# Who splits the weight tiles of a two-layer encoder: tiles moved between VectorE, GpSimd and ScalarE

## The chip, the cores and the metric

The kernel runs on one core of a Trainium2 chip. The metric is the device time in microseconds; the median of three runs of the kernel before is 1931.53 us (1929.2, 1931.96 and 1931.53).

## The reference

Two layers over 256 tokens of 1024 channels, all in float32:

```
hn = rmsnorm(x, norm1_g);  q, k, v, hy_in, gates = split(hn @ w_in)
a_out = neighbourhood_attention(rmsnorm(q), rmsnorm(k), v, rpb)      # 8 heads of 64
b_out = hyena_mixer(short_conv(hy_in), filters)                      # long convolution by FFT
x = x + (g0 * (a_out @ w_up_na) + g1 * (b_out @ w_up_hy)) @ w_out    # g0, g1: sigmoid gates
h = rmsnorm(x, norm2_g);  q = h @ peer_wq                            # scores against 2 x 128 subkeys a head
x = x + sum over the 16 chosen experts of each head of weight * gelu(h . u_tab[e]) * v_tab[e]
```

The kernel does not gather experts: it computes `h . u` for all 16384 rows of the first table, weights them by a dense matrix of routing weights, and multiplies by all of the second table.

## The kernel before, in words

**Tiles.** All weights of a layer come as one stream of 328 tiles of 128 x 1024 float32 (512 KB), numbered from 0: 0 to 7 for q and k, 8 to 11 for v, 12 to 23 for the Hyena input, 24 to 39 for the gates (`T_GATE`), 40 to 47 for the two up projections (`T_UP`), 48 to 55 for the output projection (`T_OUT`), 56 to 71 for the expert queries (`T_WQ`), 72 to 199 for the first expert table (`T_U`), and 200 to 327 for the second (`T_VT`). Everything before tile 72 is called the trunk here, 72 to 199 the first-table stage, 200 to 327 the second-table stage.

**Ring.** A tile lives in one of four slots (`RING`): `ring` (float32, where the DMA lands), `w_hi` and `w_lo` (fp16). TensorE multiplies in fp16: each product is w_hi x a_hi + w_hi x a_lo + w_lo x a_hi, three matmuls, so 24 matmuls of 256 columns for a normal tile and 12 of 512 columns for a tile of the second table.

**How a tile is split.** ScalarE makes `w_hi` = fp16(4096 x ring) (`high_part`, L504). The low half is 4096 x ring - w_hi, and there are two ways to it. For tiles 0, 1 and 204 to 327, VectorE does it in one instruction (`low_part`, L897). For tiles 2 to 203, ScalarE scales the ring slot in place (`scale_tile`, L510), and GpSimd then subtracts (`scaled_low`, L462). `POOL_TILES` = 204 is where the one way ends and the other begins.

**What orders the work.** Each engine has one list of instructions, written out by hand, which it does in order and in which it waits on semaphores. A slot goes round in a loop: the DMA of tile t + 4 is issued on SyncE when `w_lo` of tile t is made (`refill`); ScalarE makes `w_hi` of tile t + 4 when it has landed and TensorE is done with tile t (`high_wait`), and in the trunk it does this "behind" whatever it does for the results of tile t (`split_behind`); TensorE starts tile t + 4 when its low half is there (`parts_ready`). One counter, `lo_ready`, counts the low halves of all engines, so that tile order is kept across engines: GpSimd's first tile of a layer waits for VectorE's two, and VectorE's tile 204 waits for GpSimd's 203.

**Around the change in the trunk.** The sum of squares of x goes VectorE, TensorE (`mean_square`), ScalarE (the root, L544), VectorE (`inverse_rms`, L923 and on), and then in four steps between VectorE (`make_h` L958, `h_low` L966) and ScalarE (`norm_high`, L613); TensorE waits for the last of them before the v tiles (L1699). In the gate tiles VectorE does the short convolution (`conv`, L1146 to L1150, three instructions for each of twelve blocks), the scores (L1156, L1159) and the softmax's division (L1167), each waited for by TensorE's transposes (L1786).

**Around the change between the tables.** In the last tiles of the first table ScalarE evaluates gelu (`late_gelu`, L822), splits the next tile, and makes the first four expert columns' high halves (`expert_high`, L813). VectorE multiplies gelu by the routing weight (`store_late`, L1480). GpSimd, after its last weight tile, makes the columns' low halves (`expert_low`, L476). TensorE's first second-table product (L1992) needs the first column's low half and tile 200's low half; its second half needs the stores up to the third last.

## Time and profile before

| | value |
|---|---|
| runs, median | 1931.53 us |
| profiled execution, its own time | 1929.89 us |
| its span, first to last instruction | 1927.8 us |
| PE (TensorE matmul) busy | 1873.0 us, 97% |
| ACT (ScalarE) busy | 1355.3 us, 70% |
| DVE (VectorE) busy | 1218.7 us, 63% |
| POOL (GpSimd) busy | 1035.3 us, 54% |
| mean granted TensorE clock | 0.993 |

The profile names engines PE, PEld (weight loads), DVE, ACT, POOL and SP, and L12 is line 12 of the kernel. Layer 0 runs from 0 to about 961 us, layer 1 from there to the end, with nearly the same pattern.

### The profile page before, as it was taken

How to read it: one execution, taken by the hardware profiler on the slowest of the kernel's cores; microseconds unless marked ns; L12 is line 12 of the kernel's file. 1: busy time of each engine (PE TensorE's matmuls, PEld its weight loads, DVE VectorE, ACT ScalarE, POOL GpSimd, SP SyncE). 2: the span in 40 equal slices, each digit the busy share in tenths (PEclk: the TensorE clock that was granted, in tenths of full speed). 3: DMA queues.
4: the chain of work that ended last, by engine and by line, in shares of the span. 5: the costliest groups of instructions: out<-in, count | busy, mean ns of one | idle time of the engine just before them, and what ended most of it. 6: DMA issues, size and time to landing. Idle time of an engine off the chain costs nothing.

```text
span 1927.8 us, 42946 instructions
## 1 busy us (share of the span) xinstructions
PE 1873.0 (97%) x14238; PEld 1353.3 (70%) x14238; DVE 1218.7 (63%) x2530; ACT 1355.3 (70%) x1929; POOL 1035.3 (54%) x664
## 2 busy tenths in 40 slices
PE   7989999999999999999989899999999989999999
PEld 5777898899998344444457778988999974444444
DVE  5897569777775344444458974796777744444444
ACT  8787988887777455555588879888877765555554
POOL 4655868876667322222256558687776672222221
PEclk8999999999999999999999999999999999999999
DMA  8544656655555566666565446556555555656654
GB/s 265 164 143 142 214 168 201 202 188 173 174 174 167 173 205 203 200 206 200 192 213 167 143 135 227 173 197 201 192 171 167 173 175 175 206 201 202 206 198 140
DMA packets 100324, 357.38 MB, mean 185 GB/s; under 512 B 11744, under 2 KB 13730, under 8 KB 99492
## 3 DMA queue, kind: packets, MB, share of 16 engines
q1 hardware_dynamic: 99828, 354.36, 55.9%
q10 hardware_dynamic: 432, 2.18, 0.3%
q8 instruction: 39, 0.64, 0.1%
q14 instruction: 25, 0.20, 0.0%
HBM read 355.45 MB, written 1.05 MB: 185 GB/s over the span
## 4 chain that ended last, share of the span: by engine, by line
PE 87%; DVE 6%; ACT 5%; issue 2%; DMA 0%; SPq 0%; POOL 0%; DVEq 0%; ACTq 0%; POOLq 0%
PE bank L1992 35%; PE bank L1536 14%; PE bank L1538 14%; PE bank L1540 14%; PE bank L1931 3%; ACT w_hi L504 2%; ACT ring L510 2%; PE bank L1860 1%; DVE arena L1150 1%; DVE arena L1167 1%; PE bank L1911 1%; PE bank L1865 1%; DVE arena L1146 1%; DVE arena L1148 1%; PE bank L1699 0%
## 5 line engine op out<-in xcount | busy, mean ns | idle before, releaser
L462 POOL TENSOR_TENSOR w_lo<-ring,w_hi 128x1024 f16<-128x1024 f32 x404 | 863.9, 2140 | 396.5 <-ACT ring L510 395.9
L504 ACT ACTIVATE w_hi<-ring 128x1024 f16<-128x1024 f32 x654 | 685.0, 1047 | 38.2 <-PE bank L1540 25.2
L1536 PE MATMUL bank<-act_parts,w_hi 128*128 128x256 f16 x2560 | 698.0, 273 | 0.5 <-DVE act_parts L1268 0.5
L1540 PE MATMUL bank<-act_parts,w_lo 128*128 128x256 f16 x2560 | 697.8, 273 | 0.0
L1538 PE MATMUL bank<-act_parts,w_hi 128*128 128x256 f16 x2560 | 697.7, 273 | 0.0
L897 DVE SCALAR_TENSOR_TENSOR w_lo<-ring,w_hi 128x1024 f16<-128x1024 f32 x250 | 306.3, 1225 | 351.7 <-ACT w_hi L504 351.7
L476 POOL TENSOR_TENSOR e_lo<-arena,e_hi 128x256 f16<-128x256 f16 x256 | 171.2, 670 | 480.9 <-ACT e_hi L813 480.9
L510 ACT ACTIVATE ring<-ring 128x1024 f32<-128x1024 f32 x404 | 424.2, 1050 | 0.0
L1992 PE MATMUL bank<-w_hi,e_hi 128*128 128x512 f16 x1024 | 390.3, 381 | 11.3 <-issue 11.3
L1992 PE MATMUL bank<-w_lo,e_hi 128*128 128x512 f16 x1024 | 390.2, 381 | 0.0
L1992 PE MATMUL bank<-w_hi,e_lo 128*128 128x512 f16 x1024 | 389.9, 381 | 0.0
L813 ACT ACTIVATE e_hi<-arena 128x256 f16 (+1 forms) x256 | 105.9, 416 | 318.8 <-PE bank L1992 318.8
L1536 PEld LDWEIGHTS bank<-act_parts,w_hi 128*128 128x128 f16 x2560 | 250.4, 98 | 37.9 <-issue 6.4
L1540 PEld LDWEIGHTS bank<-act_parts,w_lo 128*128 128x128 f16 x2560 | 250.4, 98 | 28.9
L1538 PEld LDWEIGHTS bank<-act_parts,w_hi 128*128 128x128 f16 x2560 | 250.5, 98 | 28.4
L1992 PEld LDWEIGHTS bank<-w_hi,e_hi 128*128 128x128 f16 x1024 | 100.6, 98 | 133.5 <-issue 14.3
L1992 PEld LDWEIGHTS bank<-w_hi,e_lo 128*128 128x128 f16 x1024 | 100.7, 98 | 122.2 <-issue 2.5
L1992 PEld LDWEIGHTS bank<-w_lo,e_hi 128*128 128x128 f16 x1024 | 100.6, 98 | 121.5 <-issue 1.9
L1472 DVE SCALAR_TENSOR_TENSOR arena<-arena,bank 128x512 f32 (+1 forms) x128 | 79.4, 683 | 72.8 <-PE bank L1931 72.8
L822 ACT ACTIVATE bank<-bank 128x256 f32<-128x256 f32 x136 | 50.0, 368 | 104.0 <-PE bank L1540 98.1
L1536 PE MATMUL bank<-raw_hi,w_hi 128*128 128x256 f16 x352 | 97.4, 277 | 3.0 <-POOL w_lo L462 3.0
L1540 PE MATMUL bank<-raw_hi,w_lo 128*128 128x256 f16 x352 | 97.4, 277 | 0.0
(258 smaller groups left out, 1862.1 us busy)
## 6 DMA issues: line engine op xcount, KB each, us to landing
ring<-stream SPq DMA_DIRECT2D x654, 512.0 KB, 3.3
arena<-rpb_in SPq DMA_DIRECT2D x8, 512.0 KB, 6.2
arena<-subkeys ACTq DMA_DIRECT2D x2, 1024.0 KB, 5.6
ring<-stream SPq DMA_DIRECT2D x4, 256.0 KB, 4.8
xT<-x_in SPq DMA_DIRECT2D x4, 256.0 KB, 5.2
arena<-w_in SPq DMA_DIRECT2D x2, 512.0 KB
arena<-decay_in SPq DMA_DIRECT2D x2, 512.0 KB
arena<-dft_in SPq DMA_DIRECT2D x2, 512.0 KB, 4.3
```

The costliest lines, as they stand in the source:

```text
L462: pool.tensor_tensor(w_lo[:, slot, :], ring[:, slot, :], w_hi[:, slot, :], ALU.subtract).then_inc(lo_ready.sem, 1)
L476: pool.tensor_tensor(e_lo[:, n % RING, :], experts[:, bass.ds(i * RING + n, 1), :].rearrange("p a t -> p (a t)"), e_hi[:, n % RING, :], AL ...
L504: nc.scalar.activation(w_hi[:, slot, :], ring[:, slot, :], ACT.Copy, scale=TABLE_SCALE).then_inc(hi_ready.sem, 1)
L510: nc.scalar.activation(ring[:, slot, :], ring[:, slot, :], ACT.Copy, scale=TABLE_SCALE).then_inc(ring_scaled.sem, 1)
L813: nc.scalar.activation(e_hi[:, n % RING, :], experts[:, bass.ds(i * RING + n, 1), :].rearrange("p a t -> p (a t)"), ACT.Copy).then_inc(e_h ...
L897: V.scalar_tensor_tensor(w_lo[:, slot, :], ring[:, slot, :], TABLE_SCALE, w_hi[:, slot, :], ALU.mult, ALU.subtract).then_inc(lo_ready.sem, 1)
L1472: V.scalar_tensor_tensor(w, w, EXPERT_SCALE / WEIGHT_SCALE, bank[ROUTE_BANKS[n]][:, :].rearrange("p (t j) -> p j t", t=TOK), ALU.mult, ALU ...
L1536: T.matmul(out_, weights(w_hi, tile, j), hi[:, k, :], start=start, stop=False, skip_group_check=True)
L1538: T.matmul(out_, weights(w_hi, tile, j), lo[:, k, :], start=False, stop=False, skip_group_check=True)
L1540: return T.matmul(out_, weights(w_lo, tile, j), hi[:, k, :], start=False, stop=stop, skip_group_check=True)
L1931: ins = T.matmul(bank[ROUTE_BANKS[n]][:, t * NK:(t + 1) * NK], onehot_i[:, n % BURST, t // 2, :, t % 2], weighted_j[:, n % BURST, t // 2, ...
L1992: ins = T.matmul(bank[4 + 2 * half + tt][:, :], e_[:, slot, tokens], w_[:, slot, columns], start=first and w_ is w_hi and e_ is e_hi, stop ...
```

## The change

VectorE makes the low halves of a layer's first six tiles and of the whole second table (200 to 327 rather than 204 to 327), each in its one instruction. For tiles 6 to 55 ScalarE no longer scales the ring slot: GpSimd does it in place and then subtracts. For tiles 56 to 199 all is as before. The single counter becomes two, one for VectorE's low halves and one for GpSimd's, and whoever waits for a tile waits on the counter of its maker, by a count of that maker's tiles.

```diff
-POOL_TILES = T_VT + RING
+VECTOR_HEAD = 6
+def made_by_vector(tile):
+    return tile < VECTOR_HEAD or tile >= T_VT
+def scaled_by_pool(tile):
+    return VECTOR_HEAD <= tile < T_WQ
+def lows_by_engine(tile):               # how many low halves its maker has made up to this tile
+    return sum(made_by_vector(t) == made_by_vector(tile) for t in range(tile + 1))
...
+        def low_wait(eng, l, i, tile):  # SyncE's refills and TensorE's parts_ready
+            made = low_by_vector if made_by_vector(tile) else low_by_pool
+            eng.wait_ge(made.sem, made.at(l, i * RING + lows_by_engine(tile)))
...
         @block.gpsimd
-            def scaled_low(l, i, tile):
+            def pool_low(l, i, tile):
                 slot = tile % RING
-                pool.wait_ge(ring_scaled.sem, ring_scaled.at(l, i * RING + (tile + 1 - HEAD)))
+                if scaled_by_pool(tile):
+                    pool.wait_ge(hi_ready.sem, hi_ready.at(l, tile + 1))
+                    scaled[0] += 1
+                    pool.tensor_scalar(ring[:, slot, :], ring[:, slot, :], TABLE_SCALE, None, ALU.mult
+                                       ).then_inc(pool_scaled, 1)
+                    pool.wait_ge(pool_scaled, scaled[0])
+                else:
+                    pool.wait_ge(ring_scaled.sem, ring_scaled.at(l, i * RING + scaled_by_scalar(tile)))
                 pool.tensor_tensor(w_lo[:, slot, :], ring[:, slot, :], w_hi[:, slot, :], ALU.subtract
-                                   ).then_inc(lo_ready.sem, 1)
+                                   ).then_inc(low_by_pool.sem, 1)
             def pool_layer(l):
-                pool.wait_ge(lo_ready.sem, lo_ready.at(l, HEAD))
-                for tile in range(HEAD, RING):
-                    scaled_low(l, 0, tile)
-                with pool.Fori(1, POOL_TILES // RING) as i:
+                for tile in range(VECTOR_HEAD, T_U):
+                    pool_low(l, 0, tile)
+                with pool.Fori(0, NK // RING) as i:
...
             def scale_tile(tile):
+                if not made_by_vector(tile) and not scaled_by_pool(tile):
                     nc.scalar.activation(ring[:, slot, :], ring[:, slot, :], ACT.Copy, scale=TABLE_SCALE
                                          ).then_inc(ring_scaled.sem, 1)
...
         @block.vector                       # dve_layer, the sum of squares
                         raw_low_pair(b)
                         if not l:
                             head_low(b % 2, b // 2)
+                        elif b % 2:
+                            low_part(l, 0, HEAD + b // 2)
                 for b in range(KT // 2):
                     add_squares(b, pair_sum, bank[6 + b % 2][:, :])
+                    if not l and b % 2:
+                        low_part(l, 0, HEAD + b // 2)
...
                 V.memset(u_pad[:, :, S + 1:S + 2], 0.0)
+                for tile in range(RING, VECTOR_HEAD):
+                    low_part(l, 0, tile)
                 inverse_rms(1)
...                                         # the end of the first table
                 burst(TGROUPS // RING - 1, False)
+                low_part(l, 0, T_VT)
                 store_late(0, LATE - 3)
-                dve.wait_ge(lo_ready.sem, lo_ready.at(l, POOL_TILES))
+                low_part(l, 0, T_VT + 1)
                 for n in range(LATE - EDGE, LATE):
                     store_late(0, n, last_fresh)
-                with dve.Fori(0, (TILES - POOL_TILES) // RING) as i:
+                    low_part(l, 0, T_VT + RING + n - LATE)
+                with dve.Fori(1, NK // RING) as i:
                     for s in range(RING):
-                        low_part(l, i, POOL_TILES + s)
+                        low_part(l, i, T_VT + s)
```

On ScalarE the calls of `scale_tile` go for tiles 2 to 55 and 200 to 203 and nothing is put in their place. SyncE issues the same loads in the same order.

## Rows read from the trace of the kernel before

**Rows 1.** The page's chain of waits by engine, and the chain of 26:206 us.

```profile
PE 87%; DVE 6%; ACT 5%; issue 2%; DMA 0%; SPq 0%; POOL 0%; DVEq 0%; ACTq 0%; POOLq 0%
...
by line: ACT w_hi L504 7.9%; ACT ring L510 7.3%; PE bank L1536 7.0%; PE bank L1540 6.7%; PE bank L1538 6.6%; PE bank L1860 5.6%; issue 5.1%; DVE arena L1150 4.7%; DVE arena L1167 4.4%; DVE arena L1146 2.9%; DVE arena L1148 2.7%; PE bank L16
```

**Rows 2.** PE's waits: waiter, releaser, us in total, times, longest.

```profile
PE bank L1992 <- issue: 11.3, 2, 5.7
PE bank L1786 <- DVE arena L1167: 9.4, 6, 1.9
PE bank L1699 <- DVE act_parts L966: 7.5, 2, 4.4
...
PE bank L1536 <- POOL w_lo L462: 3.0, 2, 2.8
...
PE bank L1574 <- issue: 2.5, 2, 1.9
```

**Rows 3.** Groups by line and form: busy us, mean ns, idle before.

```profile
L462 POOL TENSOR_TENSOR w_lo<-ring,w_hi 128x1024 f16<-128x1024 f32 x404 | 863.9, 2140 | 396.5 <-ACT ring L510 395.9
...
L510 ACT ACTIVATE ring<-ring 128x1024 f32<-128x1024 f32 x404 | 424.2, 1050 | 0.0
...
L897 DVE SCALAR_TENSOR_TENSOR w_lo<-ring,w_hi 128x1024 f16<-128x1024 f32 x250 | 306.3, 1225 | 351.7 <-ACT w_hi L504 351.7
L476 POOL TENSOR_TENSOR e_lo<-arena,e_hi 128x256 f16<-128x256 f16 x256 | 171.2, 670 | 480.9 <-ACT e_hi L813 480.9
```

**Rows 4.** Timeline between the tables, layer 0: start, us, what, idle before.

```profile
617.29 2.13 POOL L462 TENSOR_TENSOR w_lo<-ring,w_hi 128x1024 f16<-128x1024 f32 x1 [0.49 <-ACT ring L510]
...
617.84 1.05 ACT L504 ACTIVATE w_hi<-ring 128x1024 f16<-128x1024 f32 x1
...
622.35 1.32 ACT L813 ACTIVATE e_hi<-arena 128x256 f16<-128x256 f32 x4
...
625.94 4.31 POOL L462 TENSOR_TENSOR w_lo<-ring,w_hi 128x1024 f16<-128x1024 f32 x2 [1.28 <-ACT ring L510]
630.21 1.92 POOL L476 TENSOR_TENSOR e_lo<-arena,e_hi 128x256 f16<-128x256 f16 x3
```

**Rows 5.** Windows: us, PE, PEld, DVE, ACT, POOL busy, PEclk, DMA share, GB/s.

```profile
625.30:630.98 5.68, 0.01 (x2) 0.04 (x2) 0.70 (x2) 2.75 (x4) 4.97 (x4) 0.91 0.54 184
630.98:636.25 5.27, 5.27 (x13) 1.87 (x14) 0.06 (x1) 0.00 (x0) 1.77 (x3) 0.50 0.31 103
...
1587.92:1592.91 4.99, 4.99 (x13) 1.81 (x14) 0.06 (x1) 0.00 (x0) 1.78 (x3) 0.54 0.32 105
```

**Rows 6.** ACT by line in 24:45.6 us, the ring's group.

```profile
L510 ACT ACTIVATE ring<-ring 128x1024 f32<-128x1024 f32 x6 | 6.8, 1128 | 0.0
```

**Rows 7.** Window of the first v tile, layer 0, columns as in Rows 5.

```profile
40.32:45.62 5.30, 5.30 (x16) 1.72 (x20) 4.67 (x9) 1.66 (x2) 3.05 (x2) 0.50 0.95 284
```

**Rows 8.** Timeline of DVE and POOL in the gate tiles.

```profile
103.07 0.74 DVE L1167 TENSOR_SCALAR arena<-arena,soft 128x256 f32<-128x256 f32 x2
...
106.04 0.48 DVE L1148 SCALAR_TENSOR_TENSOR arena<-arena,cols_sb 128x256 f32<-128x256 f32 x1
106.56 2.31 DVE L1150 SCALAR_TENSOR_TENSOR arena<-arena,cols_sb 128x256 f32<-128x256 f32 x1
...
106.46 2.13 POOL L462 TENSOR_TENSOR w_lo<-ring,w_hi 128x1024 f16<-128x1024 f32 x1 [0.61 <-ACT ring L510]
```

**Rows 9.** DVE and POOL by line in 98.4:132.45 us.

```profile
L1150 DVE SCALAR_TENSOR_TENSOR arena<-arena,cols_sb 128x256 f32<-128x256 f32 x6 | 8.3, 1389 | 0.2
L1167 DVE TENSOR_SCALAR arena<-arena,soft 128x256 f32<-128x256 f32 x10 | 7.8, 777 | 0.4
L1146 DVE TENSOR_SCALAR arena<-arena,cols_sb 128x256 f32<-128x256 f32 x6 | 5.7, 955 | 0.0
L1148 DVE SCALAR_TENSOR_TENSOR arena<-arena,cols_sb 128x256 f32<-128x256 f32 x6 | 4.8, 798 | 0.2
...
L462 POOL TENSOR_TENSOR w_lo<-ring,w_hi 128x1024 f16<-128x1024 f32 x10 | 21.4, 2137 | 15.4 <-ACT ring L510 15.4
```

More of the change, by code:

```diff
@@ L89, with scaled_by_scalar @@
 PI_BELOW = 3.1415925
+def made_by_vector(tile):
[4 more added lines that the diff above has]
+    return sum(made_by_vector(t) == made_by_vector(tile) for t in range(tile + 1))
+def scaled_by_scalar(tile):
+    return sum(not made_by_vector(t) and not scaled_by_pool(t) for t in range(tile + 1))
 class Signal:
@@ L272, in encoder_kernel @@
         hi_ready = sig("hi_ready", TILES)
-        ring_scaled = sig("ring_scaled", POOL_TILES - HEAD)
-        lo_ready = sig("lo_ready", TILES)
+        ring_scaled = sig("ring_scaled", scaled_by_scalar(TILES - 1))
+        low_by_vector = sig("low_by_vector", lows_by_engine(TILES - 1))
+        low_by_pool = sig("low_by_pool", lows_by_engine(T_VT - 1))
+        pool_scaled = sem("pool_scaled")
         tile_done = sig("tile_done", TILES)
@@ L365, in load, with refill @@
                              ).then_inc(ring_full[slot].sem, 16)
-            def refill(turn, slot):
-                sp.wait_ge(lo_ready.sem, turn * RING + (slot + 1 - RING))
-                load(turn * RING + slot, slot)
+            def refill(l, i, group, slot):
+                tile = (group - 1) * RING + slot
+                if group:
+                    low_wait(sp, l, i, tile)
+                else:
+                    low_wait(sp, l - 1, i, TILES + tile)
+                load(i * RING + (l * TILES + group * RING + slot), slot)
             def layer_loads(l):
@@ L400, in layer_loads @@
                 for slot in range(RING):
-                    refill(l * GROUPS + 1, slot)
+                    refill(l, 0, 1, slot)
                     taps(slot)
                 for slot in range(RING):
-                    refill(l * GROUPS + 2, slot)
+                    refill(l, 0, 2, slot)
                     if slot == 0:
@@ L410, in layer_loads @@
                     for slot in (2 * (r % 2), 2 * (r % 2) + 1):
-                        refill(l * GROUPS + 3 + r // 2, slot)
+                        refill(l, 0, 3 + r // 2, slot)
                         if slot % 2 == 0:
                             offsets(r)
-                with sp.Fori(l * GROUPS + 5, (l + 1) * GROUPS) as turn:
+                with sp.Fori(0, T_VT // RING + 1 - 5) as i:
                     for slot in range(RING):
-                        refill(turn, slot)
+                        refill(l, i, 5, slot)
+                with sp.Fori(0, GROUPS - 1 - T_VT // RING) as i:
+                    for slot in range(RING):
+                        refill(l, i, T_VT // RING + 1, slot)
             def load_x(b):
@@ L442, in _ @@
                     for slot in range(RING):
-                        refill((l + 1) * GROUPS, slot)
+                        refill(l + 1, 0, 0, slot)
             def store(n, b, tokens):
@@ L509, in scale_tile @@
                 slot = tile % RING
-                nc.scalar.activation(ring[:, slot, :], ring[:, slot, :], ACT.Copy, scale=TABLE_SCALE
-                                     ).then_inc(ring_scaled.sem, 1)
+                if not made_by_vector(tile) and not scaled_by_pool(tile):
+                    nc.scalar.activation(ring[:, slot, :], ring[:, slot, :], ACT.Copy, scale=TABLE_SCALE
+                                         ).then_inc(ring_scaled.sem, 1)
             def head_high(tile, half):
@@ L786, in act_layer @@
                     norm_high(2, (s,))
-                with act.Fori(2, (T_U - T_WQ) // RING) as w:
-                    for s in range(RING):
-                        high_part(l, w, T_WQ + s + RING)
-                        scale_tile(T_WQ + s + RING)
+                for tile in range(T_WQ + 3 * RING, T_U + RING):
+                    high_part(l, 0, tile)
+                    scale_tile(tile)
                 for n in range(8):
@@ L836, in act_layer @@
                     late_gelu(0, n)
-                with act.Fori(0, TGROUPS // RING) as i:
+                with act.Fori(0, TGROUPS // RING - 1) as i:
                     for s in range(RING):
                         late_gelu(i, EDGE + s)
+                for n in range(LATE - EDGE - RING, LATE - EDGE):
+                    late_gelu(0, n)
                 for n in range(LATE - EDGE, LATE):
@@ L897, in low_part @@
                 V.scalar_tensor_tensor(w_lo[:, slot, :], ring[:, slot, :], TABLE_SCALE, w_hi[:, slot, :],
-                                       ALU.mult, ALU.subtract).then_inc(lo_ready.sem, 1)
+                                       ALU.mult, ALU.subtract).then_inc(low_by_vector.sem, 1)
             def head_low(tile, half):
@@ L908, in head_low @@
                                        w_hi[:, tile, columns], ALU.mult, ALU.subtract
-                                       ).then_inc(lo_ready.sem if half else head_lo[tile], 1)
+                                       ).then_inc(low_by_vector.sem if half else head_lo[tile], 1)
             def dve_layer(l):
@@ L1525, in parts_ready @@
                 def parts_ready(i, tile):
-                    pe.wait_ge(lo_ready.sem, lo_ready.at(l, i * RING + (tile + 1)))
+                    low_wait(pe, l, i, tile)
                 def weights(part_, tile, k):
@@ L2001, in v_last @@
                 pe.wait_ge(e_lo_ready.sem, e_lo_ready.at(l, n + 1))
-                pe.wait_ge(lo_ready.sem, lo_ready.at(l, T_VT + n + 1))
+                low_wait(pe, l, 0, T_VT + n)
                 ins = v_half(n, half, False, n == NK - 1)
```

8 lines of the change are left out of this document (3 added, 5 removed).

## The prediction

> **What bounds the kernel now.** I read the chain of waits first. By engine it is 87% PE, 6% DVE, 5% ACT and 2% issue [rows 1]: TensorE sets the time nearly everywhere, and a change to the splitting of tiles can only win where PE stands still or runs slowly. PE's own waits say where that is [rows 2]. The largest is one gap of 5.7 us per layer ahead of the first second-table product, which the view can only name "issue" because several semaphores meet there. Then come the gate tiles, where PE waits six times for VectorE's softmax division (9.4 us in all), the v tiles, where it waits for the last low half of the normalised activations (7.5 us in two gaps, the longest 4.4), tile 2 or 4 of a layer, which waits for GpSimd's low half (3.0, the longest 2.8), and the sum of squares (2.5). The chain of 26 to 206 us, the trunk of layer 0 after its start, tells who stands behind these gaps: ScalarE's in-place scaling has 7.3% of its 180 us, 13.1 us, and VectorE's convolution and division have 14.7%, 26.5 us [rows 1]. The first is what this change takes off ScalarE; the second is what GpSimd can make worse.
>
> **Part 1, between the tables.** The 5.7 us gap is a queue on GpSimd. Its list has the low halves of tiles 200 to 203 ahead of the expert columns' low halves. The last two of them run from 625.94 for 4.31 us, and only then, at 630.21, does L476 begin; its first column takes 0.67 us, and PE starts at 630.98. The columns' high halves had been ready since 622.35 + 1.32 = 623.67 [rows 3, 4]. The change takes the four tiles off that list. GpSimd's last subtraction in the stage is then tile 199's, which ends at 617.29 + 2.13 = 619.4, so the column can be split at about 622.8 and is there long before PE is done with the first table at 625.30 [rows 5]. What is late next? Tile 200's low half, on VectorE: 1.23 us [rows 3], after w_hi (617.84 + 1.05 = 618.9 [rows 4]) and after GpSimd's 619.4, thus by 621. The later three, with one store each, have 2.6 us per tile. So the whole gap goes: 2 x 5.68 = 11.3 us [rows 2, 5]. More goes with it. After the gap PE is granted half its clock: the first 13 matmuls take 5.27 us at a granted 0.50 in layer 0 and 4.99 us at 0.54 in layer 1 [rows 5]. At full clock they would take 5.27 x 0.50 = 2.64 and 4.99 x 0.54 = 2.69 us, which gives back 2.6 and 2.3. Part 1 is worth 11.3 + 4.9 = 16.2 us. Its bounds: at least 11.3, if the slow clock comes anyhow; nothing, if another wait takes the gap's place (a rival below).
>
> **Part 2, starts of the layers and the normalisation.** VectorE's one instruction (1.23 us) replaces ScalarE's 1.05 and GpSimd's 2.14 for tiles 2 to 5 [rows 3]. The low half comes about 2 us sooner after w_hi, but VectorE has to fit it between the sums of squares. In layer 0 I count 0.7 us sooner at tile 2 (of the wait of 2.8) and 0.6 at the sum of squares, in layer 1 about 2.4 us through both (its wait there is 1.9, and two scalings less go before it) [rows 2]: the root starts 1.3 and 2.4 us sooner. Then ScalarE is the limit up to the v tiles. It does six scalings there, 6.8 us [rows 6], between the steps of the normalisation; without them VectorE's own steps become the limit and I take 2.5 us of the 6.8 per layer. Bounds: 0 and all 6.8. So the v tiles start 3.8 and 4.9 us sooner. In layer 0 the first v tile also runs at a granted 0.50 for 5.30 us [rows 7]; with a gap of under 2 us instead of 4.35 I expect it at full clock, 2.6 us more.
>
> **What GpSimd then costs.** The trace has no scaling on GpSimd. The subtraction with two inputs takes 2.14 us for 1024 columns and 0.67 for 256 [rows 3]: 0.18 fixed and 1.91 ns a column. One input instead of two bounds it from below at the fixed part and half the slope, 1.16 us, from above at the subtraction's 2.14. ScalarE's 1.05 for the same work is close to the lower end, and I take 1.16. GpSimd then needs 1.16 + 2.14 and two hand-overs, 3.4 us per tile, where PE needs 2.6. While the v and the first Hyena tiles come back to back, GpSimd becomes the pacer, and of the 6.4 and 4.9 us won by the first v tile some 1 us per layer is lost again by the next point at which VectorE is the limit (the second sine argument). Part 2: 5.5 + 3.5 = 9 us.
>
> **Part 3, VectorE is locked out in the gate tiles.** A convolution instruction takes 0.48 us when GpSimd stands still (the row at 106.04) and 2.31 us when GpSimd's subtraction began 0.10 us before it (106.56 against 106.46) [rows 8]: it waits until the subtraction has ended. The same is seen at L1146, L1148 and L1167, whose inputs all lie in SBUF, and not at those that read PSUM. In 98.4 to 132.45 us, where VectorE is the chain, these four groups hold 8.3 + 7.8 + 5.7 + 4.8 = 26.6 us; free they would hold 18 x 0.48 + 10 x 0.37 = 12.3. So 14 us of 34 are waits for ten subtractions, 1.4 us each [rows 8, 9]. The change gives GpSimd ten more instructions in this stretch, of 1.16 us. In the same proportion each costs 0.77 us; some will fall beside the PSUM work, and I take 0.7: 7 us per layer, 14 us in all. Bounds: 0, if they all fall beside other work, and 1.9 each, if each blocks for its whole length and the subtraction behind it now does so too, 38 us. ScalarE's relief does not help here, since it is not in this chain.
>
> The Trainium skill says this of the mechanism (SBUF — State Buffer, "Who interferes with whom"): VectorE and GpSimd share one pair of SBUF ports, an instruction of VectorE with two SBUF inputs or in a two-port mode collides with a GpSimd instruction that reads SBUF, and whichever comes second is blocked for the other's whole length. By this rule, the trace agrees: 2.31 us instead of 0.48. It speaks against the change, because it makes the upper bound above, not the proportion, the natural price.
>
> **Part 4, the rest.** Of the 13.1 us of scaling in the chain per layer [rows 1] some 4.5 belong to part 2; of the other 8.6, which lie mostly between the last heads and the up projections, a parallel path on VectorE is nearly as late, so 2.5 per layer is what I count: 5 us won. More lock-outs in the filters: 1 us per layer lost. At the output projection GpSimd's tiles come at PE's 2.6 us and now need 3.4 each; it starts with some 4 us in hand (the ring's lead) and falls 0.8 behind per tile over five tiles, so about 0.5 us per layer. For the second table VectorE gets four tiles more per layer, beside PE at its full rate: nothing.
>
> **Sum.** -16.2 (part 1) - 9 (part 2) + 14 (part 3) - 5 + 2 + 1 (part 4) = -13.2 us. Against the profiled execution's own 1929.9 us (1927.8 of span) that is 1916.7; the median of the runs is 1.6 above that execution, so I forecast 1918 us.
>
> **Rivals.**
> *GpSimd becomes the bound of the trunk (slower).* Tiles 6 to 55 are 50 low halves in the 180 us from 26 to 206, 3.6 us each. At 1.16 us a scaling they need 3.4 and pass; from 1.3 us on they don't. At 2.14, the subtraction's length, 50 x 4.4 = 220 us: 40 per layer more, less the ring's lead of about 4, and part 2 is gone: 1929.9 + 72 - 16 = 1986. At 1.5 us 190 us are needed, 10 more per layer less the lead, with part 2 gone and part 3 larger: about 1936. For it: the margin is thin. Against it: the fit of rows 3 and ScalarE's 1.05.
> *Each new instruction blocks in full (slower).* Part 3 costs its upper bound: 38 us instead of 14, thus 1942. For it: instructions of VectorE follow each other within 0.04 us there, so one is always waiting. Against it: only 1.4 of 2.14 us was lost per subtraction so far.
> *The locks cost little (faster).* If scaling and subtraction fall in one pause of VectorE, and ScalarE's relief counts in full in part 4, part 3 costs 6 and part 4 wins 8: 1907.
> *The gap between the tables stays.* Another of the waits that meet there (the stores, tile 200 on VectorE) is as late: 1918 + 16 = 1934. The stamps of rows 4 speak against it.
>
> **How the numbers follow.** My forecast has 0.50, the cheap locks 0.22, GpSimd as the bound 0.13, full blocking 0.10, the gap that stays 0.05. A difference of 0.2%, 3.9 us, is what can be told from none here. The first two are faster; of GpSimd as the bound a small part still is; so 0.76 faster, 0.06 the same, 0.18 slower. The range goes from 1903, below the cheap locks, to 1940, which takes in full blocking nearly and the mild form of the bound; it leaves out the heavy form. The likeliest case alone has 1910 to 1926.
>
> **What would show it.** The gap ahead of L1992 and the half clock after it are gone, in both layers. GpSimd's scaling is 1.1 to 1.3 us long. PE's wait at L1699 falls from 7.5 us to under 5. In the gate tiles L1146 to L1150 and L1167 hold more time (part 3), and PE waits longer than 9.4 us at L1786. PE waits for `w_lo` of GpSimd now and then, under 5 us a layer. The forecast is wrong if such waits grow past 10 us per layer, or if the gate tiles take over 10 us per layer more.

## The result, and the profile after

The changed kernel takes 2063.24 us (median of 4 runs, 2062.33 to 2065.05) where the kernel before takes 1931.35: 1.0686 times as long, interval 1.0668 to 1.0705. The forecast was 1918 us with a range of 1903 to 1940; both the sign and the range were wrong. The profiled execution took 2063.48 us, its span is 2061.2.

The page first. Lines are by the numbers of the changed kernel: L500 is GpSimd's scaling, L505 its subtraction, L553 ScalarE's scaling, L937 VectorE's low half, L1584 to L1588 the products, L2040 the second table (L1992 before).

```profile
PE 1906.1 (92%) x14238; PEld 1363.6 (66%) x14238; DVE 1232.3 (60%) x2546; ACT 1257.8 (61%) x1813; POOL 1285.0 (62%) x748
...
PE 73%; POOL 24%; issue 1%; DMA 1%; ACT 1%; DVE 0%; SPq 0%; DVEq 0%; ACTq 0%
```

In the chain of waits GpSimd went from 0% to 24% of the span [rows 1]. Yet it is busy only 62% of the whole: the mean hides that it is busy nearly all the time in the two trunks. The window of the first one (columns as in Rows 5) and PE's waits (waiter, releaser, us, times, longest) show it:

```profile
26.00:290.00 264.00, 191.12 (x1436) 143.81 (x1435) 139.60 (x251) 111.14 (x191) 255.48 (x104) 0.93 0.36 116
```

```profile
PE bank L1584 <- POOL w_lo L505: 103.3, 68, 4.0
PE bank L1913 <- POOL w_lo L505: 20.7, 12, 2.3
PE bank L1747 <- POOL w_lo L505: 11.1, 7, 2.3
```

The waits of [rows 2] are nearly all replaced by one, for GpSimd's low half: 135.1 us in these three rows, 139.5 with a fourth at L1908. The gap of 5.7 us ahead of the second table is gone. Even PE's busy time is 33 us longer than before (1906.1 against 1873.0) for the same 14238 matmuls. The granted clock in this window is 0.93, where the trunk before (26 to 206 us) had 0.98.

The groups by line answer [rows 3]:

```profile
L505 POOL TENSOR_TENSOR w_lo<-ring,w_hi 128x1024 f16<-128x1024 f32 x388 | 831.1, 2144 | 217.2 <-ACT ring L553 208.5
...
L937 DVE SCALAR_TENSOR_TENSOR w_lo<-ring,w_hi 128x1024 f16<-128x1024 f32 x266 | 327.2, 1230 | 346.5 <-ACT w_hi L546 346.5
...
L500 POOL TENSOR_SCALAR ring<-ring 128x1024 f32<-128x1024 f32 x100 | 278.7, 2787 | 61.8 <-ACT w_hi L546 53.6
```

The scaling takes 2.79 us. The prediction took 1.16 and held 2.14 for the upper bound. GpSimd's timeline shows the two in turn with no idle time but the hand-over of 0.09 us:

```profile
67.22 2.77 POOL L500 TENSOR_SCALAR ring<-ring 128x1024 f32<-128x1024 f32 x1
70.07 2.12 POOL L505 TENSOR_TENSOR w_lo<-ring,w_hi 128x1024 f16<-128x1024 f32 x1
72.28 2.77 POOL L500 TENSOR_SCALAR ring<-ring 128x1024 f32<-128x1024 f32 x1
```

From 67.22 to 72.28 is 5.06 us per tile, where the trunk before took 3.6. For comparing kernels by stage I read from each trace when the last product of a tile ends, and add the two layers (us; each row is one profiled execution):

| tiles | 0-7 | 8-15 | 16-23 | 24-39 | 40-55 | 56-71 | 72-199 | 200-327 |
|---|---|---|---|---|---|---|---|---|
| before | 65.9 | 59.7 | 57.5 | 123.6 | 104.5 | 85.0 | 745.0 | 681.5 |
| changed | 71.6 | 80.2 | 84.9 | 163.0 | 159.3 | 87.4 | 745.0 | 664.8 |
| junction alone (e1) | 66.0 | 61.2 | 57.4 | 123.6 | 104.5 | 85.0 | 745.0 | 664.8 |
| no scaling on GpSimd (e2) | 61.4 | 62.5 | 57.5 | 123.6 | 104.5 | 85.0 | 745.0 | 664.8 |
| no scaling at all (e9) | 58.8 | 52.1 | 56.9 | 119.2 | 100.0 | 85.0 | 745.0 | 664.8 |
| half subtraction (e8) | 61.3 | 61.7 | 73.1 | 143.7 | 100.0 | 87.6 | 745.0 | 664.8 |
| two-operation scaling (e12) | 61.4 | 61.3 | 73.0 | 142.4 | 100.0 | 86.7 | 745.0 | 664.8 |
| gate tiles on VectorE (e11) | 59.3 | 63.5 | 57.5 | 110.6 | 103.6 | 85.0 | 745.0 | 664.8 |
| e11 and two-operation scaling (e13) | 63.4 | 60.4 | 69.4 | 109.5 | 100.0 | 86.3 | 745.0 | 664.8 |

In the changed kernel tiles 8 to 55 take 487.4 us over both layers: 96 tiles at 5.08. Whatever a stage needs, v, Hyena, gate or up, GpSimd's 5.06 us sets it. Only the second table gained, 16.7 us.

The first column is the least certain: e5, described below, is the same program as e2 up to the end of GpSimd's list and has 58.8 us there where e2 has 61.4. And e9's row is from the fastest of its five runs, 4.3 us under its median.

### The profile page after: what moved, and what is told of

It reads as the page before. It is cut to its first block, busy times and chain, and to the rows that moved or that the text cites. A ratio compares the mean times of both kernels' runs of the same rounds, so it can differ in the third digit from the quotient of the medians.

```text
span 2061.2 us, 42886 instructions
## 1 busy us (share of the span) xinstructions
PE 1906.1 (92%) x14238; PEld 1363.6 (66%) x14238; DVE 1232.3 (60%) x2546; ACT 1257.8 (61%) x1813; POOL 1285.0 (62%) x748
## 3 DMA queue, kind: packets, MB, share of 16 engines
HBM read 355.45 MB, written 1.05 MB: 173 GB/s over the span
## 4 chain that ended last, share of the span: by engine, by line
PE 73%; POOL 24%; issue 1%; DMA 1%; ACT 1%; DVE 0%; SPq 0%; DVEq 0%; ACTq 0%
PE bank L2040 32%; POOL ring L500 13%; PE bank L1584 12%; PE bank L1586 12%; PE bank L1588 12%; POOL w_lo L505 11%; PE bank L1979 3%; DMA ring<-stream 1%; PE bank L1959 1%; ACT w_hi L546 0%; DVE w_lo L937 0%; ACT raw_hi L612 0%; PE bank L2065 0%; SPq L454 0%; SPq L458 0%
## 5 line engine op out<-in xcount | busy, mean ns | idle before, releaser
L505 POOL TENSOR_TENSOR w_lo<-ring,w_hi 128x1024 f16<-128x1024 f32 x388 | 831.1, 2144 | 217.2 <-ACT ring L553 208.5
L1584 PE MATMUL bank<-act_parts,w_hi 128*128 128x256 f16 x2560 | 704.6, 275 | 89.9 <-POOL w_lo L505 88.8
L1588 PE MATMUL bank<-act_parts,w_lo 128*128 128x256 f16 x2560 | 704.7, 275 | 0.0
L937 DVE SCALAR_TENSOR_TENSOR w_lo<-ring,w_hi 128x1024 f16<-128x1024 f32 x266 | 327.2, 1230 | 346.5 <-ACT w_hi L546 346.5
L2040 PE MATMUL bank<-w_hi,e_hi 128*128 128x512 f16 x1024 | 388.1, 379 | 0.0
L2040 PE MATMUL bank<-w_lo,e_hi 128*128 128x512 f16 x1024 | 388.1, 379 | 0.0
L2040 PE MATMUL bank<-w_hi,e_lo 128*128 128x512 f16 x1024 | 388.1, 379 | 0.0
L1584 PEld LDWEIGHTS bank<-act_parts,w_hi 128*128 128x128 f16 x2560 | 252.5, 99 | 139.6 <-issue 102.9
L500 POOL TENSOR_SCALAR ring<-ring 128x1024 f32<-128x1024 f32 x100 | 278.7, 2787 | 61.8 <-ACT w_hi L546 53.6
L553 ACT ACTIVATE ring<-ring 128x1024 f32<-128x1024 f32 x288 | 301.5, 1047 | 0.0
L1588 PEld LDWEIGHTS bank<-act_parts,w_lo 128*128 128x128 f16 x2560 | 252.8, 99 | 31.6
L2040 PEld LDWEIGHTS bank<-w_hi,e_lo 128*128 128x128 f16 x1024 | 100.2, 98 | 120.8
L2040 PEld LDWEIGHTS bank<-w_lo,e_hi 128*128 128x128 f16 x1024 | 100.2, 98 | 120.4
L2040 PEld LDWEIGHTS bank<-w_hi,e_hi 128*128 128x128 f16 x1024 | 100.2, 98 | 120.4
L1584 PE MATMUL bank<-raw_hi,w_hi 128*128 128x256 f16 x352 | 98.4, 280 | 12.4 <-POOL w_lo L505 9.0
```

The source lines that it names most:

```text
L500: pool.tensor_scalar(ring[:, slot, :], ring[:, slot, :], TABLE_SCALE, None, ALU.mult).then_inc(pool_scaled, 1)
L505: pool.tensor_tensor(w_lo[:, slot, :], ring[:, slot, :], w_hi[:, slot, :], ALU.subtract).then_inc(low_by_pool.sem, 1)
L553: nc.scalar.activation(ring[:, slot, :], ring[:, slot, :], ACT.Copy, scale=TABLE_SCALE).then_inc(ring_scaled.sem, 1)
L937: V.scalar_tensor_tensor(w_lo[:, slot, :], ring[:, slot, :], TABLE_SCALE, w_hi[:, slot, :], ALU.mult, ALU.subtract).then_inc(low_by_vector ...
L1584: T.matmul(out_, weights(w_hi, tile, j), hi[:, k, :], start=start, stop=False, skip_group_check=True)
L1588: return T.matmul(out_, weights(w_lo, tile, j), hi[:, k, :], start=False, stop=stop, skip_group_check=True)
```

## The experiments

Each ratio is to the kernel before, run on the same chip. The theory at the start: GpSimd's scaling is the whole loss, and all the rest of the change gains.

**e1, the junction alone.** VectorE makes 200 to 203; the head is as before.

```diff
-VECTOR_HEAD = 6
+VECTOR_HEAD = HEAD
-    return VECTOR_HEAD <= tile < T_WQ        # scaled_by_pool
+    return False
...
```

The rest of the edit puts ScalarE's calls for tiles 2 and 3 back and takes VectorE's low halves of tiles 2 to 5 out.

> Only the junction between the tables is changed: VectorE makes the low halves of tiles 200 to 203 too; everything else is as in the kernel before. My theory (GpSimd's scaling alone made the change slow, and the rest of it gains): the gap of 5.7 us and the half clock behind it go in both layers, 1931.4 - 16 = 1915 us; 1920 if the half clock stays (only 11.3 won). Rival (another wait takes the gap's place, and the moved low halves are worth nothing or cost): 1931 or above.

1915.49 us, ratio 0.9921 [0.9908, 0.9935]: 15 us won. Part 1 is right.

**e2, all but GpSimd's scaling.** Only the second of these edits.

> The whole change but for GpSimd's scaling: VectorE makes tiles 0 to 5 and 200 to 327, ScalarE scales 6 to 199 as before. Theory (GpSimd's scaling is the whole loss): all but 2 to 5 us of the prediction's part 2 comes on top of part 1, 1909 to 1914 us, thus 149 to 154 us below the changed kernel. Rival (the head on VectorE costs too: low halves between the sums of squares delay the root of the normalisation): above the kernel with the junction alone, 1918 to 1925. Rival (the counters and the order of the new waits cost): anything far above 1931.

1911.48 us, 0.9901 [0.9886, 0.9916]. VectorE's head gains 4 us more (tiles 0 to 7: 61.4 instead of 66.0). The changed kernel's excess over it, 152 us, is all due to who scales tiles 6 to 55.

**e6, extra work in the gate tiles.**

```diff
+                if T_GATE <= tile < T_UP:
...
+                    pool.tensor_tensor(e_lo[:, slot, :], mats[:, 0:2, :].rearrange("p a k -> p (a k)"),
+                                       w_hi[:, slot, 0:S], ALU.subtract)
                 pool.tensor_tensor(w_lo[:, slot, :], ring[:, slot, :], w_hi[:, slot, :], ALU.subtract
```

> The kernel without GpSimd's scaling, with one more two-input instruction of GpSimd (256 columns and 256 columns from SBUF, some 0.67 us, its result unused) ahead of the subtraction of each of the 16 gate tiles (24 to 39), 32 in all. GpSimd has room for it there (0.67 + 2.14 = 2.8 us per tile in a stage where VectorE's chain takes 3.4 us). It measures the price of an added GpSimd instruction beside VectorE's convolution. Proportional (part 3's rule, 1.4 us lost per 2.14 of GpSimd: 0.66 of its length): some 20 of them fall in the stretch that VectorE sets, 20 x 0.44 = 9 us slower than the same kernel without them. Full blocking: 20 x 0.67 = 13 us. Free: within 2 us. If the hand-overs add their own time to GpSimd's path, more than 13.

1910.79 us, 0.9898 [0.9882, 0.9913]: free. The convolution and division groups hold 90.7 us instead of 87.6 over both layers, and PE does not see it. This spoke for cheap lock-outs, and it misled: the longer instructions of e8 (1.23 us) and e12 (1.08 us) are not free.

**e7 and e10, the dose.** GpSimd scales the even tiles (e7) or every third (e10), ScalarE the others.

```diff
-    return VECTOR_HEAD <= tile < T_WQ
+    return VECTOR_HEAD <= tile < T_WQ and tile % 2 == 0      # e10: tile % 3 == 0
```

> The changed kernel with GpSimd scaling only the even tiles of 6 to 55 (25 per layer instead of 50); ScalarE scales the odd ones. Theory (GpSimd's rate is the cause: it is the bound once its mean time per tile passes the 3.6 us of the trunk): (5.05 + 2.2) / 2 = 3.6 us per tile, right at the break-even, so some 0 to 20 us per layer over the kernel without scaling, 1915 to 1950 us. Rival (each scaling adds its price in a chain, through the lock-outs of VectorE or the late refills, with no threshold): half of the changed kernel's loss of about 150 us, 1985 us.

> The changed kernel with GpSimd scaling only every third tile of 6 to 55 (17 per layer). Theory (a rate bound): (5.05 + 2 x 2.2) / 3 = 3.15 us per tile, under the trunk's 3.6, and the ring's lead takes up the single long tile: 1908 to 1916 us. Rival (each scaling costs its share): from the half dose's 26.8 us over the kernel without scaling, 2/3 of it, 1929; from the full dose's 152, a third, 1962.

e7: 1938.3 us, 1.0041 [1.0027, 1.0055]. e10: 1924.68 us, 0.9978 [0.9966, 0.9989]. Over e2 that is 13 us for a third of the scalings, 27 for half, 152 for all. The steep part is the rate; but below the break-even the cost is not zero, as the theory had it. Something else costs 13 us at a third of the dose. The trace of e10 says where: against e2 it loses 14.3 us in tiles 16 to 23 and 12.3 in the gate tiles, and wins 11.6 in tiles 8 to 15. In the filters VectorE's low halves (L1167) take 2.15 us each, 0.72 in e2, and PE waits there (L1782) for VectorE 11.4 us, 3.1 in e2. PE's waits for GpSimd's low halves are 4.5 us in all, so most of the loss comes through VectorE and not from a late GpSimd.

**e9, no scaling of tiles 6 to 55 at all,** on either engine.

```diff
-                    scaled[0] += 1
-                    pool.tensor_scalar(ring[:, slot, :], ring[:, slot, :], TABLE_SCALE, None, ALU.mult
-                                       ).then_inc(pool_scaled, 1)
-                    pool.wait_ge(pool_scaled, scaled[0])
```

> The changed kernel without any scaling of tiles 6 to 55, on either engine (left out: the multiplication by 1024 of these tiles); GpSimd waits for the high half and subtracts. It shows what ScalarE's relief alone is worth, the most that moving the scaling anywhere could bring. The prediction counted 2.5 us of the normalisation and 2.5 us in the later stages per layer, 10 in all: 1911.5 - 10 = 1901 us. Rival (ScalarE's scaling lies beside other work nearly everywhere): 1908 to 1912. If the chain's 13.1 us of 180 per layer were all real: 1886.

1893.45 us (1889.13 to 1899.32), 0.9825 [0.9812, 0.9839]. ScalarE's relief is worth 18 us over e2 by the medians, 22.5 by the two profiled executions, not 10: in the table 10.4 in tiles 8 to 15, 4.4 in the gate tiles, 4.5 in the up and output tiles, and the rest in the first column and the filters.

**e8, the prediction's own price.** In place of the scaling GpSimd makes the first half of the columns of the subtraction, which it then does again in full. The kernel leaves out the scaling of tiles 6 to 55, as e9 does.

```diff
-                    pool.tensor_scalar(ring[:, slot, :], ring[:, slot, :], TABLE_SCALE, None, ALU.mult
-                                       ).then_inc(pool_scaled, 1)
+                    pool.tensor_tensor(w_lo[:, slot, 0:D // 2], ring[:, slot, 0:D // 2], w_hi[:, slot, 0:D // 2],
+                                       ALU.subtract).then_inc(pool_scaled, 1)
```

> The changed kernel at the price that the prediction took: in place of the scaling of tiles 6 to 55 GpSimd makes the first 512 columns of the subtraction (by the fit of rows 3, 0.18 + 512 x 1.91 ns = 1.16 us) and waits for it as it waited for the scaling; ScalarE doesn't scale these tiles either. Left out: the scaling by 1024 of these tiles. Theory (only the price of the scaling was wrong, the sum holds for its own price): 1918 us, between 1910 and 1926. Rival (the margin is too thin: with bunched tiles 3.4 us per tile already paces the trunk): 1925 to 1945. Rival (added GpSimd work is free up to its rate, as the extra instructions in the gate tiles were): 1900 to 1908, that is ScalarE's relief without part 3's 14 us.

1941.77 us, 1.0059 [1.0045, 1.0072], with 1.23 us per instruction. So with the size right (nearly) the forecast would still have been wrong, by 24 us: a second error.

**e4, two inputs for the scaling.** `scale_row` is one constant per partition, read again for every column.

```diff
-                    pool.tensor_scalar(ring[:, slot, :], ring[:, slot, :], TABLE_SCALE, None, ALU.mult
+                    pool.tensor_tensor(ring[:, slot, :], ring[:, slot, :], scale_row, ALU.mult
```

> The changed kernel with GpSimd's scaling written as a two-input multiplication (second input one constant per partition, read again for every column). Theory (the one-input instruction with a constant is the slow form, 2.77 us, and two inputs take the subtraction's 2.14): 2.14 + 2.14 and hand-overs = 4.4 us per tile, 0.63 less for 100 tiles, 2000 us. Rival (what is slow is a 4-byte result, twice the bytes of the subtraction's, whatever the form): 2.77 us or more again, 2063 us or above.

1993.32 us, 1.0334 [1.032, 1.0348]. The two-input product takes less time than the one-input scaling, 1.97 us, with a 4-byte result:

```profile
L503 POOL TENSOR_TENSOR ring<-ring,scale_col 128x1024 f32<-128x1024 f32 x100 | 197.0, 1970 | 76.5 <-ACT w_hi L551 76.5
```

**e5, single instructions of GpSimd** on e2, behind its last subtraction, beside and after the kernel's last products.

```diff
...
+            for n in (D, D // 2, D // 4, D):
+                link(pool.tensor_scalar(A[:, 0:n], A[:, 0:n], TABLE_SCALE, None, ALU.mult))       # L541
+            link(pool.tensor_scalar(B, A, TABLE_SCALE, None, ALU.mult))                           # L542
+            link(pool.tensor_scalar(A, A, TABLE_SCALE, 1.0, ALU.mult, ALU.add))                   # L543
+            link(pool.tensor_scalar(C, A, 1.0, None, ALU.mult))                                   # L544
+            link(pool.tensor_copy(B, A))                                                          # L545
+            link(pool.tensor_tensor(A, A, B, ALU.mult))                                           # L546
...
```

`link` makes each instruction wait for the one before.

> The kernel without GpSimd's scaling, and behind GpSimd's last piece of work a list of single GpSimd instructions on an unused part of SBUF, each waiting for the one before; the output is untouched. In order: memset; one-input scaling in place of 1024, 512, 256 and 1024 columns of 128 partitions; scaling into another place; scaling and adding; scaling to half-width results; a plain copy; three two-input operations of 1024 columns (product of two tiles, product with one constant per partition, subtraction with a half-width result); the same subtraction of 512. Theory (the one-input form with a constant is slow in itself, by some 2.6 ns a column, because 4-byte results or the constant are handled slower): 2.77 at 1024 in every scaling with 4-byte results, half at 512; the plain copy near 1.2. Rival (the 2.77 comes from the kernel around it, where VectorE and the transfers use the same memory): 1.2 to 2.1 us when alone. Rival (working in place is what costs): less into another place. The products with 4-byte results tell whether the result's width costs: 2.1 if not, 2.8 if so.

1919.21 us in its one run. The probe's groups by form:

```profile
L541 POOL TENSOR_SCALAR arena<-arena 128x1024 f32<-128x1024 f32 x2 | 5.8, 2884 | 0.2
L542 POOL TENSOR_SCALAR arena<-arena 128x1024 f32<-128x1024 f32 x1 | 2.8, 2770 | 0.1
L544 POOL TENSOR_SCALAR arena<-arena 128x1024 f16<-128x1024 f32 x1 | 2.8, 2769 | 0.1
L546 POOL TENSOR_TENSOR arena<-arena 128x1024 f32<-128x1024 f32 x1 | 2.3, 2338 | 0.1
...
L541 POOL TENSOR_SCALAR arena<-arena 128x512 f32<-128x512 f32 x1 | 1.5, 1491 | 0.1
...
L543 POOL TENSOR_SCALAR arena<-arena 128x1024 f32<-128x1024 f32 x1 | 1.0, 1047 | 0.1
L545 POOL COPY arena<-arena 128x1024 f32<-128x1024 f32 x1 | 1.0, 1037 | 0.1
```

The 2.77 us is the form's own: outside the trunk, into another place, and with half-width results it stays. Both rivals fall, and so does the theory's guess about 4-byte results or the constant: the line to read is L543. With a second operation, an addition, the same instruction on the same data takes 1.05 us, as long as a plain copy. Slow is the scaling with one operation and none in the second place.

**e12, the changed kernel with the fast form.**

```diff
-                    pool.tensor_scalar(ring[:, slot, :], ring[:, slot, :], TABLE_SCALE, None, ALU.mult
+                    pool.tensor_scalar(ring[:, slot, :], ring[:, slot, :], TABLE_SCALE, 0.0, ALU.mult, ALU.add
```

> The changed kernel, with GpSimd's scaling written with two operations (times 1024, plus 0.0) instead of one. Alone and in place, multiplying and adding took 1.05 us for 1024 columns where multiplying alone took 2.77. Theory (that price is the whole error of the forecast): GpSimd needs 1.05 + 2.14 and hand-overs, 3.35 us per tile, and the forecast's own 1918 us holds, between 1905 and 1926. Rival (added GpSimd work of this length still locks VectorE out in the filters and gate tiles as the half subtractions of 1.23 us did): 1930 to 1942. Rival (one-input instructions hold VectorE hardly at all, as in the changed kernel, whose 52 convolution and division instructions per layer took no longer than before, so that nearly all of ScalarE's relief is kept): 1895 to 1905. Rival (the form is fast only alone): 2060.

1939.03 us, 1.0042 [1.0027, 1.0057]. One more operation in the instruction makes the kernel 124 us faster. In place the scaling takes 1.08 us:

```profile
L500 POOL TENSOR_SCALAR ring<-ring 128x1024 f32<-128x1024 f32 x100 | 108.4, 1084 | 111.6 <-ACT w_hi L546 105.1
```

But the forecast's 1918 is missed by 21 us, and e8's 1942 is nearly met: what is left depends on GpSimd's added time, not on its number of inputs. PE's waits say where:

```profile
PE bank L1834 <- DVE arena L1213: 23.0, 6, 5.3
PE bank L1782 <- DVE arena L1175: 11.4, 2, 5.7
PE bank L1635 <- issue: 5.6, 2, 3.9
```

In e9 these three, at its L1830, L1778 and L1631, are 8.2, 2.5 and 0.4 us. The first two releasers are VectorE. VectorE's timeline in the gate tiles beside GpSimd's:

```profile
104.32 2.31 DVE L1194 SCALAR_TENSOR_TENSOR arena<-arena,cols_sb 128x256 f32<-128x256 f32 x1
106.66 1.14 DVE L1196 SCALAR_TENSOR_TENSOR arena<-arena,cols_sb 128x256 f32<-128x256 f32 x1
```

```profile
104.22 2.13 POOL L505 TENSOR_TENSOR w_lo<-ring,w_hi 128x1024 f16<-128x1024 f32 x1
106.43 1.10 POOL L500 TENSOR_SCALAR ring<-ring 128x1024 f32<-128x1024 f32 x1
107.61 2.17 POOL L505 TENSOR_TENSOR w_lo<-ring,w_hi 128x1024 f16<-128x1024 f32 x1
```

The row at 104.32 is held by the subtraction, and the next one, at 106.66, by the scaling, which ends at 107.53: it takes 1.14 us for work of 0.48. Each GpSimd instruction holds VectorE until it ends, one after the other, and a step of VectorE's chain passes between them.

The view names no releaser for the third wait, but in the program TensorE waits there for the second sine argument (layer 0, tiles 8 to 15), whose last step is L1041. The timeline shows the same locks in it:

```profile
51.15 1.09 DVE L1038 TENSOR_SCALAR arena<-arena 128x128 f32<-128x128 f32 x1
52.28 2.24 DVE L1039 SCALAR_TENSOR_TENSOR arena<-arena 128x128 f32<-128x128 f32 x1
54.55 1.08 DVE L1040 SCALAR_TENSOR_TENSOR arena<-arena 128x128 f32<-128x128 f32 x1
55.67 2.11 DVE L1041 TENSOR_SCALAR arena<-arena 128x128 f32<-128x128 f32 x1
```

```profile
57.88 2.09 PE L1635 MATMUL bank<-arena 32*128 32x256 f32 x16 [3.92 <-issue]
```

L1041 ends at 57.78, and L1635 starts 0.10 us later. Where nothing holds them these four steps take 0.23, 0.29, 0.29 and 0.23 us (in e9, from 37.98 us). The five steps L1037 to L1041 take 7.9 us here and 3.7 in the same place of e9.

**e11, VectorE makes the gate tiles' low halves.** SyncE's refills and GpSimd's list leave these tiles' counters to VectorE; 16 calls of `low_part` go between its steps.

```diff
-    return tile < VECTOR_HEAD or tile >= T_VT
+    return tile < VECTOR_HEAD or T_GATE <= tile < T_UP or tile >= T_VT
...
                     if tiles:
                         conv(tiles.pop(0))
+                    low_part(l, 0, low[0])
                     normalise_probs(2 * p + 1)
```

> The kernel without GpSimd's scaling, with VectorE making the low halves of the 16 gate tiles too (24 to 39, one instruction of 1.23 us each, put between its convolution, score and division steps); ScalarE scales and GpSimd subtracts only the other tiles. Theory (a GpSimd subtraction costs VectorE's chain in the gate tiles 1.4 us through the lock-out, by rows 8 and 9, and ScalarE's scaling costs something too): VectorE pays 1.23 instead of 1.4 per tile, 16 x 0.17 = 2.7 us per layer, and ScalarE's relief there adds some 2 per layer (what the kernel without any scaling gained in this stage): 1911.5 - 9 = 1902 us, not under 1898. Rival (the lock-outs lie beside waits of VectorE that stay, so the added 1.23 us come on top): up to 16 x 1.23 = 20 us per layer slower, 1920 to 1950.

1897.15 us, 0.9828 [0.9815, 0.9842]: the fastest version that leaves nothing out, 33 us under the kernel before (1930.16 beside it) and 166 under the changed one. It won 14 us over e2, more than the 9 of the theory, 13.0 of it in the gate tiles. The lock-outs there are gone to the last one: no convolution or division step takes over 0.49 us. The groups of its convolution (L1196 to L1200) and division (L1217):

```profile
L1200 DVE SCALAR_TENSOR_TENSOR arena<-arena,cols_sb 128x256 f32<-128x256 f32 x24 | 11.6, 485 | 0.9
L1198 DVE SCALAR_TENSOR_TENSOR arena<-arena,cols_sb 128x256 f32<-128x256 f32 x24 | 11.6, 485 | 0.9
L1217 DVE TENSOR_SCALAR arena<-arena,soft 128x256 f32<-128x256 f32 x32 | 11.3, 353 | 1.1
L1196 DVE TENSOR_SCALAR arena<-arena,cols_sb 128x256 f32<-128x256 f32 x24 | 9.8, 408 | 0.1
```

That is 44.3 us for the 104 instructions, against 107.6 in e12, whose rows follow, 91.6 in e9 and 87.6 before. ScalarE's relief has a part in the 13.0 us that was not separated; without any scaling (e9) it won 4.4 there.

```profile
L1213 DVE TENSOR_SCALAR arena<-arena,soft 128x256 f32<-128x256 f32 x32 | 37.6, 1175 | 1.1
L1194 DVE SCALAR_TENSOR_TENSOR arena<-arena,cols_sb 128x256 f32<-128x256 f32 x24 | 25.6, 1066 | 0.9
L1192 DVE TENSOR_SCALAR arena<-arena,cols_sb 128x256 f32<-128x256 f32 x24 | 23.1, 962 | 0.1
L1196 DVE SCALAR_TENSOR_TENSOR arena<-arena,cols_sb 128x256 f32<-128x256 f32 x24 | 21.3, 886 | 0.9
```

**e13, both:** e11, and GpSimd scales its tiles 6 to 23 and 40 to 55 with two operations.

> VectorE makes the low halves of the gate tiles, as in the kernel with that alone (1897 us), and GpSimd scales (times 1024, plus 0.0) and subtracts tiles 6 to 23 and 40 to 55, so that ScalarE scales nothing before tile 56. Theory (ScalarE's scaling is on the path between the v tiles and the filters, 5.2 and 6.7 us in the two layers by the kernel without scaling, and 1.8 per layer after the gate tiles; GpSimd has room for 1.05 us more): 1897 - 15 = 1882, with some 2 to 8 us of lock-outs in the filters 1884 to 1890. Rival (GpSimd's 3.35 us per tile and its lock-outs in the filters take back the relief, 10 to 15 us over both layers by the half-subtraction kernel): 1895 to 1900 or slower.

1905.88 us, 0.988 [0.9865, 0.9894]: 9 us slower than e11. The stage table splits it: 3.6 won in tiles 40 to 55, 3.1 in 8 to 15, 1.1 in the gate tiles, but 11.9 lost in 16 to 23, the filters, 4.1 in tiles 0 to 7 (of which some 2 to 3 us can be the difference between two executions, as e5 and e2 show) and 1.3 in 56 to 71. The rival was right. Scaling on GpSimd in tiles 40 to 55 alone would by this table give 2 to 3 us over e11; it was not tried.

## Why the prediction was wrong

**The step that failed by far the most: "One input instead of two bounds it ... from above at the subtraction's 2.14".** The scaling takes 2.79 us, outside both bounds. That one term costs 124 us (2063.2 against e12's 1939.0). The step assumed that an instruction with fewer inputs cannot take longer. ScalarE's 1.05 was no evidence for GpSimd. The first rival, GpSimd as the bound of the trunk, is what happened, and its formula holds at the measured size: 50 x 5.07 = 253.5 us per layer, 73.5 more than 180, less 4 of lead, twice, less 16, gives 2053, 10 us under the measured time. It had 0.13 and a time of 1986, because it was worked out at the false upper bound, and the range left it out.

**Part 1 held.** -16.2 forecast, -15 measured (e1), -16.7 in the table. At the junction of the changed kernel the first 27 matmuls run at the full clock (window, columns as in Rows 5):

```profile
700.20:705.47 5.27, 5.27 (x27) 2.43 (x25) 3.15 (x4) 2.69 (x4) 1.60 (x2) 1.00 0.70 226
```

**Part 2 and ScalarE's relief were too small.** VectorE's work for tiles 2 to 5 gave 4 (e2 against e1) and ScalarE's relief 18 (e9 against e2), 22 us in all; I had 11.3 by the v tiles and 5 later, 16.3.

**Part 3's mechanism was right, its price too low, and a place was missed.** At the true 1.08 us, adding the scalings to e9 costs 45.6 us (e12). I had 14 for the gate tiles and 5.3 elsewhere (2 in the filters, 1 at the output projection, 2.3 in the v tiles). In the table: gate tiles 23.2, filters 16.1, v and first Hyena tiles 9.2, head 2.6, tiles 56 to 71 1.7, up and output tiles nothing (52.8 together; the two profiled spans differ by 52.5, the medians by 45.6). In the filters VectorE's low halves (two inputs in SBUF) take 1.98 us each instead of 0.69, and PE's wait there grows by 9 us. Part 3 had looked only at the gate tiles; the second sine argument I had named, but priced at 1 us per layer. I took "0.7 us each" in proportion to the share lost so far. With the right length of the scaling the forecast would thus have missed by these terms: 26 us too little for GpSimd's work, 6 too little for what tiles 2 to 5 and ScalarE's relief win, 1 too much for part 1. Together that is 21 us, which is what e12 is above 1918.

The rival "each new instruction blocks in full", with 0.10, has the mechanism right: the rows of e12 show steps that are held to the end of the scaling. Its 1942, beside 1939 (e12) and 1942 (e8), is in part luck. It put 38 us on the gate tiles, which measured 23.2, and left the forecast's 5 on the other stages, which measured 29.6.

In the sum over the changed kernel part 3 doesn't show: the 104 instructions hold 87.5 us, as before. There the slow scaling holds VectorE only for its first part. In the two timelines a convolution step that arrives with it takes 1.20 us, and the two behind it run in their own 0.48 beside its remaining 1.5 us:

```profile
125.03 1.20 DVE L1192 TENSOR_SCALAR arena<-arena,cols_sb 128x256 f32<-128x256 f32 x1
126.26 0.48 DVE L1194 SCALAR_TENSOR_TENSOR arena<-arena,cols_sb 128x256 f32<-128x256 f32 x1
126.78 0.48 DVE L1196 SCALAR_TENSOR_TENSOR arena<-arena,cols_sb 128x256 f32<-128x256 f32 x1
```

```profile
125.05 2.77 POOL L500 TENSOR_SCALAR ring<-ring 128x1024 f32<-128x1024 f32 x1
```

A step that comes 0.23 us after the start of a slow scaling shows it more clearly, since there is no doubt who came first:

```profile
104.92 1.14 DVE L1196 SCALAR_TENSOR_TENSOR arena<-arena,cols_sb 128x256 f32<-128x256 f32 x1
106.09 0.42 DVE L1192 TENSOR_SCALAR arena<-arena,cols_sb 128x256 f32<-128x256 f32 x1
106.54 0.48 DVE L1194 SCALAR_TENSOR_TENSOR arena<-arena,cols_sb 128x256 f32<-128x256 f32 x1
```

```profile
104.69 2.82 POOL L500 TENSOR_SCALAR ring<-ring 128x1024 f32<-128x1024 f32 x1
```

In e12 the step at 106.66 comes 0.23 us after the start of a fast scaling and takes the same 1.14 us. So in these two rows the slow form holds VectorE no longer than the fast one; the rest of its 2.82 us leaves VectorE free, and there it catches up.

The Trainium skill (SBUF — State Buffer, "Who interferes with whom") says that the second comer is blocked for the other's whole instruction. The two-input subtraction and e12's fast scaling agree (2.31 and 1.14 us for 0.48). The slow form doesn't: the step at 104.92 comes second, with 2.59 us of the scaling still to go, and has ended after 1.14. There the measurement decides.

**The signs I had named.** The gap at the second table is gone, as said. "GpSimd's scaling is 1.1 to 1.3 us long" failed at once, and "such waits grow past 10 us per layer" was met seven times over. The wait at the v tiles did not fall (11.1 us, now for GpSimd). With GpSimd as the pacer VectorE's waits vanish from the view, so the views of the changed kernel alone would not have shown the second error; it took e8 and e12.

**Still open:** why the one-operation form is slow, and why 0.67 us more in each gate tile (e6) is free while 1.08 costs 23 us over all gate tiles. GpSimd stands idle 0.6 to 2.6 us between two subtractions there; that the first fits in this pause and the second leaves VectorE none is argued, not shown. How much of e12's loss is GpSimd's rate (3.4 us per tile in stages of 3.3 to 3.7) and how much is the locks can only be bounded, by PE's waits. Between the profiled executions of e9 and e12, 52.5 us apart, the waits for VectorE's division grow by 14.8 us, those in the filters by 8.9, the one behind the sine argument by 5.2, and the waits for GpSimd's low half from nothing to 6.5 (5.0 at L1584, 1.5 at L1747). PE's busy time grows by 19.4 us, at a granted clock of 0.988 instead of 1.000; which of the waits brought that on was not separated.

## What to carry to other kernels

Bound an instruction form that the trace doesn't hold by a probe, not by its neighbours: the neighbour with more inputs was no upper bound, and a second operation made the form 2.6 times as fast. Where GpSimd shares a stretch with a chain of short SBUF instructions on VectorE, count each added GpSimd instruction at its full length as the upper bound: 32 of 1.08 us (34.6 us of work) cost e12 23.2 us in the gate tiles. It can be cheaper to give the work to VectorE itself: in the gate tiles 1.23 us there removed a lock of 1.4 us, GpSimd's 2.14 and ScalarE's scaling of 1.05.

## What the runs showed of the hardware

- GpSimd's one-input multiplication with one operation takes 2.77 us for 128 x 1024 (1.49 for 512 columns); multiplying and adding takes 1.05, a copy 1.04. The Trainium skill (GPSIMD Engine Reference, "Engine selection") has one-input work at roughly line rate; the two-operation form and the copy agree (1.0 ns a column), the one-operation form does not (2.7 ns).
- A two-input product takes 2.34 us with two tiles, 1.89 alone and 1.97 in the kernel when the second input is one constant per partition. Every two-input form was faster than the slow one-input form.
- PE's busy time for the same 14238 matmuls went from 1859.6 us (e9) over 1865.8 (e11) and 1879.0 (e12) to 1906.1 in the changed kernel, at mean granted clocks of 1.000, 0.996, 0.988 and 0.980. The kernels in which PE waits most in the trunk have the lower clock there (0.93 in the changed kernel's first trunk, 1.00 in e9's gate tiles), so the short waits seem to cost more than their own length; no run separates the two.
- The slow scaling holds a VectorE step that reads SBUF for about its first microsecond only, as long as the fast scaling does: 1.14 us for a step of 0.48 in both, with 2.82 and 1.10 us of scaling beside it.
